# A decoder step for 520 tokens: the input of the S5 layer cut by transposes instead of selection products, the phase tables built in halves, and x loaded once

## What is computed

```python
def _s5_scan(u, h_re, h_im, ...):
    lam_bar = jnp.exp(lam * dt)
    b_bar = ((lam_bar - 1.0) / lam)[..., None] * lax.complex(b_re, b_im)
    ...
        bu = jnp.einsum('blgc,gpc->blgp', u_blk, b_bar)
        bu = bu.at[:, 0].add(lam_bar * h)
        _, hs = lax.associative_scan(_linear_combine, (a, bu), axis=1)
        y = jnp.real(jnp.einsum('blgp,gcp->blgc', hs, c_c)) + d_g * u_blk
...
x = x + mix                      # mixer output, residual
x = x + _hmoe(_rmsnorm(x, norm_ffn), ...)
```

## Time and profile before

| what | us |
|---|---|
| median of 3 runs | 1200.95 (1197.68 to 1205.63) |
| the profiled execution | 1194.14 |
| its span | 1192.3 |
| PE busy | 1025.3 (86%) |
| DVE busy | 431.6 (36%) |
| POOL busy | 333.8 (28%) |
| ACT busy | 169.9 (14%) |

### The profile page before, as it was taken

How to read it: one execution, slowest core, us unless ns; L and a number is a source line. 1 busy time by engine, 2 the same in 40 slices (tenths; PEclk the granted TensorE clock), 3 DMA queues, 4 the chain that set the end, 5 groups by cost and what they waited for, 6 DMA issues and landing times.

```text
span 1192.3 us, 16177 instructions
## 1 busy us (share of the span) xinstructions
PE 1025.3 (86%) x5932; PEld 655.4 (55%) x5932; DVE 431.6 (36%) x939; ACT 169.9 (14%) x320; POOL 333.8 (28%) x550
## 2 busy tenths in 40 slices
PE   3999998899688878888869967999997999877776
PEld 2888877666544444444438865644445555444442
DVE  3300055676542222222373069201346332222216
ACT  3201020132200000000141101200244000000002
POOL 0070000277366666566484000000000112111100
PEclk9999979899599999989985567999997799999999
...
DMA packets 53300, 288.45 MB, mean 242 GB/s; under 512 B 11867, under 2 KB 21851, under 8 KB 34535
## 3 DMA queue, kind: packets, MB, share of 16 engines
...
## 4 chain that ended last, share of the span: by engine, by line
PE 54%; DMA 29%; DVE 7%; SPq 4%; issue 2%; ACT 2%; POOL 1%; DVEq 0%; POOLq 0%; ACTq 0%
DMA arena<-in_w_gu 19%; PE ps L688 12%; PE ps L938 10%; PE ps L815 8%; PE ps L1099 5%; DMA arena<-in_w_down 4%; PE ps L1038 3%; PE ps L1040 3%; PE ps L928 2%; SPq L529 2%; DMA arena<-scratch_yd 2%; DVE arena L1480 2%; PE ps L1070 2%; PE ps L1066 2%; PE ps L845 1%
## 5 line engine op out<-in xcount | busy, mean ns | idle before, releaser
L938 PE MATMUL ps<-arena 128*64 128x256 f32 x2048 | 248.3, 398 | 64.6 <-DMA arena<-in_w_gu 62.7
L938 PEld LDWEIGHTS ps<-arena 128*64 128x64 f32 x2048 | 151.3, 142 | 163.1 <-DMA arena<-in_w_gu 55.4
L2176 POOL TENSOR_TENSOR arena<-arena 128x256 f32<-128x256 f32 (+3 forms) x192 | 132.7, 691 | 40.7 <-POOL arena L2176 40.3
L688 PE MATMUL ps<-arena 128*128 128x260 f32 x640 | 142.8, 383 | 0.0
L2110 POOL TENSOR_TENSOR arena<-arena 128x32 f32<-128x32 f32 (+5 forms) x167 | 90.5, 542 | 161.8 <-ACTq L1273 146.1
L688 PEld LDWEIGHTS ps<-arena 128*128 128x128 f32 x640 | 121.5, 191 | 20.0 <-issue 0.4
L928 PE MATMUL ps<-arena 128*64 128x512 f32 x512 | 118.8, 605 | 13.0 <-DMA arena<-in_w_down 12.5
L815 PE MATMUL ps<-arena 128*128 128x512 f32 x256 | 119.8, 620 | 2.5 <-DVE arena L1626 2.4
L1851 DVE TENSOR_TENSOR arena<-arena,ps 128x128 f32<-128x128 f32 x64 | 18.5, 289 | 276.6 <-ACT arena L1362 271.9
L2207 POOL COPY idx_now<-idx_list 128x1 int32 (+1 forms) x32 | 6.1, 191 | 308.0 <-DVEq L1766 279.5
L815 PEld LDWEIGHTS ps<-arena 128*128 128x128 f32 x256 | 62.4, 251 | 48.4 <-issue 33.0
...
## 6 DMA issues: line engine op xcount, KB each, us to landing
...
```

The costliest lines, as they stand in the source:

```text
L688: mm = pe.matmul(o[:, b, 0:HALF], w[:, kc, (n % 2) * P:(n % 2 + 1) * P], HT[:, kc, b * HALF:(b + 1) * HALF], start=kc == 0, stop=kc == KC - 1)
L938: mm = pe.matmul(ps[CAP * f:CAP * f + CAP, 2 + s, 0:256], XT[l][:, kc, CAP * s:CAP * s + CAP], WGU[l][i][s][:, kc, 256 * f:256 * f + 256], ...
L2176: g_.tensor_tensor(o, x, y, f).then_inc(sem("matrix_steps"), 1)
```

## The change

- x is loaded once, every fourth row to a tile. HT and MIX are written in the order that this asks for (HT with a stride of four elements, MIX in rows of 32 or less), and the output product reads MIX contiguously. The second load and DVE's wait for it go.
- After the experts of layer 0 the tiles are combined in the order 0, 1, 2, samples, 3. ACT makes both block forms and clears a buffer PAD before the first tile. DVE writes the normalised tiles as HX, where the 128 columns of eight groups of four tiles' channels lie together; ACT puts the samples in PAD.
- `recut` and its tables go. PE transposes PAD (16 times) and HX (32 times, in eighths), DVE copies the ends and ACT the middle of U, four copies an eighth. The product `driven` (before: zs) follows each eighth.
- POOL builds the phase table of half 0, reports, waits for the combined sample tile, and builds half 1. R8 is two buffers, filled by ACT after each report.
- SP issues all 8 reads of taps of half 0; those of half 1 are shared with ACT. The last `driven` comes behind the first `columns`. The first half of `glu` of tile 0 comes ahead of the last `turned`.
- `most` is read where it was, by each engine after its loop.

```diff
-    j += [(("k",), "act")]
-    j += [(("u", q), "act" if q % 2 else "dve") for q in range(8)]
-    j += [(("zs", q), "dve") for q in range(8)]
-    for q in range(8):
-        j += [(("y", q), "act" if q < 4 else "dve")]
-        if q >= 2:
-            j += [(("yT", q - 2), "act")]
+    j += [(("k",), "act"), (("us",), "dve"), (("u", 0), "act")]
+    for q in range(4):
+        j += [(("u", q + 1), "act"), (("zs", q), "dve")]
+    j += [(("u", q), "act") for q in (5, 6, 7)] + [(("zs", q), "dve") for q in (4, 5, 6)]
+    j += [(("y", 0), "act"), (("zs", 7), "dve"), (("y", 1), "act")]
+    for q in range(2, 8):
+        j += [(("y", q), "act" if q < 4 else "dve"), (("yT", q - 2), "act")]
...
         HC = place(A + 32928, 5, D)
-        H2 = place(A, 5, D)
+        HX = place(A, GU, TILES, CW)
...
+        R8 = [place(A + 19456 + 1024 * half, PAIRS // 2, NCH) for half in range(2)]
+        TMP = R8[1]
         KS = place(S5_AT, KC, P)
...
+        def norm_of_experts(l, t):
+            if l:
+                return X[:, t, :], HC[:, t, :], GB
+            if t == TILES:
+                return X[:, t, :], HS, GB
+            return by_group(X[:, t, :]), HX[:, :, t, :], by_group(GB)
...
             for i in range(TILES):
-                load(X[:, i, :], T["x_prompt"][i * P:(i + 1) * P, :], f"x_in_{i}")
+                load(X[:, i, :], every_fourth(T["x_prompt"], i), f"x_in_{i}")
...
-            for i in range(TILES):
-                load(X[:, i, :], every_fourth(T["x_prompt"], i), "x_again")
...
-                ring.wait_full(sp, "zs", 4 * half + 3)
-                for s in range(L // 2):
-                    taps(sp, s, half)
+            ring.wait_full(sp, "zs", 3)
+            for s in range(L):
+                taps(sp, s, 0)
+            ring.wait_full(sp, "zs", 7)
+            for s in range(L // 2):
+                taps(sp, s, 1)
...
+                        pe.wait_ge(sem("pad_ready"), 2)
...
+                                 for n in range(GU // 4)])
+            pe.wait_ge(sem("h_2"), 5)
+            rows_of_tiles = HX.rearrange("p g i c -> p (g i c)")
+
+            def in_chunks(q):
+                transposes(("u", q), [(slot("u", q)[:, 0, j * P:(j + 1) * P],
+                                       rows_of_tiles[:, (4 * q + j) * P:(4 * q + j + 1) * P]) for j in range(4)])
+
+            def driven(q):
+                if q == 0:
+                    ring.wait_emptied(pe, "us")
                 ring.wait_free(pe, "zs", q)
                 ring.wait_emptied(pe, "u", q)
...
+
+            in_chunks(0)
+            for q in range(4):
+                in_chunks(q + 1)
+                driven(q)
+            for q in (5, 6, 7):
+                in_chunks(q)
+            for q in (4, 5, 6):
+                driven(q)
+            columns(0)
+            driven(7)
+            for q in range(1, 8):
                 columns(q)
                 if q >= 2:
                     turned(q - 2)
-            for kc in (6, 7):
-                turned(kc)
-            for kc in range(KC):
-                ring.wait_emptied(pe, "yT", kc)
-
...
                     return
-                for kc in range(KC):
+                for kc in kcs:
...
-            for i in range(5):
+                if kcs[-1] == KC - 1:
+                    full(mm)
+            glu(0, range(4))
+            turned(7)
+            glu(0, range(4, KC))
+            for i in range(1, 5):
                 glu(i)
...
-        def phases(tt, m):
+        def phases(tt, half, m):
...
             ur_, ui_ = UNIT[m.bit_length() - 1]
-            c, s = TURNS[:, :, 1], TURNS[:, :, 0]
-            cmul(tt, c[:, :, :, m:2 * m], s[:, :, :, m:2 * m], c[:, :, :, 0:m], s[:, :, :, 0:m], unit(ur_), unit(ui_),
-                 temp(0, m), temp(m, 2 * m))
+            c, s = TURNS[:, half, 1], TURNS[:, half, 0]
+            cmul(tt, c[:, :, m:2 * m], s[:, :, m:2 * m], c[:, :, 0:m], s[:, :, 0:m], unit(ur_), unit(ui_),
+                 TMP[:, :, 0:m], TMP[:, :, m:2 * m])
...
-                give(act, a.copy(HT[:, :, i * P:(i + 1) * P], slot("ht", i).rearrange("p b (k n) -> p (b k) n", n=P)),
+                give(act, a.copy(HT[:, :, i:SEQ:TILES], slot("ht", i).rearrange("p b (k n) -> p (b k) n", n=P)),
                      "ht", i)
...
-                give(act, a.activation(MIX[:, g].rearrange("p (b n) -> p b n", b=2), slot("pw", g)[:, :, 0:HALF],
+                src, first = slot("pw", g), HALF // TILES
+                out = MIX[:, g, 0:SEQ].rearrange("p (i m) -> p m i", i=TILES)
+                step(a.activation(out[:, 0:first], src[:, 0, 0:HALF].rearrange("p (m i) -> p m i", i=TILES),
+                                  ACT.Copy, scale=pscale[:, g:g + 1]))
+                step(a.activation(out[:, first:P], src[:, 1, 0:SEQ - HALF].rearrange("p (m i) -> p m i", i=TILES),
+                                  ACT.Copy, scale=pscale[:, g:g + 1]))
...
+            def clear_pad(step):
+
+                step(a.copy(PAD.rearrange("p g c -> p (g c)"),
+                            before[0:XSROWS, 0:1].broadcast_to((XSROWS, 2 * D))))
+
+            def fill_pad(step):
+
+                rows_ = by_group(HS[0:NS])
+                step(a.copy(PAD[0:NS, :, CW:2 * CW], rows_))
+                a.copy(PAD[XSROWS - NS:XSROWS, :, 0:CW], rows_).then_inc(sem("pad_ready"), 1)
...
-                    tile_squares(act, 2 * l + 2, t, junk[t])
-                    tile_root(act, 2 * l + 2, t, t)
-                    if l == 0 and t < 2:
-                        make_bd(t, step)
+                if l == 0:
+                    for q in range(2):
+                        make_bd(q, step)
+                    clear_pad(step)
+                for k, t in enumerate(combined_order(l)):
+                    act.wait_ge(sem(f"combined_{l}"), k + 1)
+                    tile_squares(act, 2 * l + 2, t, JUNK[l], k)
...
+            def decays(half):
+
+                act.wait_ge(sem("phases_ready"), half + 1)
+                step(a.copy(R8[half], spread(mag8[:, PAIRS // 2 * half:PAIRS // 2 * (half + 1)], NCH)))
+                a.copy(R8[half][:, :, 0:1], zeros.unsqueeze(1).broadcast_to((P, PAIRS // 2, 1))
+                       ).then_inc(sem("decays_ready"), 1)
+
+            def u_out(q):
+                take(act, "u", q)
+                src = slot("u", q)[:, 0, :].rearrange("p (j c s) -> p s j c", j=4, s=2)
+                out = U[:, 8 * q:8 * q + 8].rearrange("p (j b) n -> p b j n", b=2)
+                for b in range(2):
+                    for s in range(2):
+                        ins = a.copy(out[64 * s:64 * s + 64, b, :, NS:SC], src[64 * b:64 * b + 64, s])
+                        if (b, s) != (1, 1):
+                            step(ins)
+                give(act, ins, "u", q)
+
+            for q in range(3):
+                u_out(q)
+            decays(0)
+            for q in range(3, 8):
+                u_out(q)
+            decays(1)
             act.wait_ge(sem("taps_out"), 16)
-            for half in range(2):
-                ring.wait_full(act, "zs", 4 * half + 3)
-                for s in range(L // 2, L):
-                    taps(act, s, half)
+            ring.wait_full(act, "zs", 7)
+            for s in range(L // 2, L):
+                taps(act, s, 1)
...
-                give(dve, v.tensor_tensor(MIX[:, H:2 * H, c * P:(c + 1) * P],
-                                          slot("hT", c)[:, 0, :].rearrange("p (h n) -> p h n", h=H),
-                                          Zo[:, :, c * P:(c + 1) * P], ALU.mult), "hT", c)
+                per = P // TILES
+                out = MIX[:, H:2 * H, 0:SEQ].rearrange("p h (i m) -> p h m i", i=TILES)
+                give(dve, v.tensor_tensor(out[:, :, per * c:per * (c + 1)],
+                                          slot("hT", c)[:, 0, :].rearrange("p (h m i) -> p h m i", h=H, i=TILES),
+                                          Zo[:, :, c * P:(c + 1) * P].rearrange("p h (m i) -> p h m i", i=TILES),
...
-                if k == 0:
-                    dve.wait_ge(sem("x_again"), 16 * TILES)
...
-            recut(dve, step, v.tensor_copy, lambda out, x, m: v.tensor_scalar(out, x, m, None, ALU.mult),
-                  lambda out: step(v.memset(out, 0.0)), 0)
-            ring.wait_full(dve, "u", 7)
+            ring.wait_full(dve, "k")
+            step(v.memset(U[:, :, 0:NS], 0.0))
+            step(v.memset(U[:, :, SC:UC], 0.0))
+            take(dve, "us")
+            src = slot("us")[:, :, 0:8 * XSROWS].rearrange("p b (n k) -> p b n k", k=XSROWS)
+            out = U.rearrange("p (b n g) k -> p g b n k", b=2, n=8)
+            for g_ in range(4):
+                rows_ = src[32 * g_:32 * g_ + 32]
+                step(v.tensor_copy(out[P - 32:P, g_, :, :, 0:NS], rows_[:, :, :, 0:NS]))
+                ins = v.tensor_copy(out[0:32, g_, :, :, SC:UC], rows_[:, :, :, XSROWS - NS:XSROWS])
+                if g_ < 3:
+                    step(ins)
+            give(dve, ins, "us")
```

(24 more changed lines are left out.)

183 lines of the change are left out of this document (80 added, 103 removed).

## The result

The changed kernel takes 1131.76 us (median of four runs, 1126.93 to 1134.85) against 1201.22 for the kernel before on the same chip: a ratio of 0.942, interval 0.937 to 0.946. It is faster by 69 us. The forecast was 1134. The profiled execution took 1131.54, its span is 1129.7; the forecast on that basis was 1127.8.

What follows compares the result with a forecast made beforehand. PE's products making U cost 71.5 us of the chain, around weight-bound expert stages. Terms summed to -66.3: 1194.1 became 1127.8, plus 6.8 for the median over the profiled run, 1134.6, stated as 1134; range 1116 to 1149.

Steps and rivals of the forecast that it cites:

- S: Start of PE's second four eighths of output in the S5 layer: 682.8 us instead of 747.10, -64.3.
- Layer 0: First layer: output product's contiguous weight loads gain 1.2 us, HT's strided write costs 0.5.
- Start of the states: First `rotated` on DVE in the S5 layer: 626 us, POOL's half table and PE level; 629 if half the cover goes.
- Half 0: First half of the S5 states on DVE: 24.8 us as before, ending at 650.8.
- the first rival: POOL and DVE slow each other fully in the S5 layer: second four eighths start at 692, total 1143; chance 0.20.
- Half 1: Second half of the S5 states on DVE: starts at 658 behind POOL's second table, ends at 682.8.
- Taps: SP's and ACT's tap reads for the S5 layer: second half's landing at 673 to 676, covered with 7 us to spare.
- the third rival: Tap reads, not tables, are last: eight take 25 us, halves there at 657 and 692, total 1144; chance 0.10.
- S to the output product: From the second four eighths through GLU: restart at half clock +2.5, reordered transposes -1.3, GLU keeping its clock -2.5.
- full contention: Same as the first rival: POOL and DVE slow each other fully, total 1143; chance 0.20.
- the table bound nothing: Rival on POOL's second phase table: DVE takes POOL's turns, PE binds at 676, total 1125; chance 0.12.
- the slower case: PE stays at 1.2 GHz behind the transposes through GLU and the output product: total 1268; chance 0.03.

Runs made afterwards that it cites:

- e11: The changed kernel as it is, run once more beside the version with all parts: 1129.83 us, ratio 0.942 to the kernel before.
- e2: The changed kernel with POOL waiting for DVE's report of the first half's states before building the second phase table: 1141.50 us, ratio 0.950, one run.
- e9: The changed kernel with POOL's sample terms held until DVE has reported the first half's states: 1123.57 us, ratio 0.938, one run.
- e1: The changed kernel with SP holding the first half's eight tap reads until DVE has reported that half's states: 1148.62 us, ratio 0.956, one run.
- e4: The changed kernel with POOL reporting both halves of its phase table only when both are built: 1147.50 us, ratio 0.954.
- e5: The changed kernel with copies moved from DVE to ACT, last states' products behind the states, and POOL's sample terms after DVE's first report: 1123.49 us, ratio 0.937.
- e6: The changed kernel with the last `driven` product moved ahead of the first `columns`, in PE's order and the PSUM slots: 1129.51 us, ratio 0.943.
- e7: The changed kernel with the edits of e5 and e6 together: 1122.64 us, ratio 0.938.

## Why the prediction was right, and where it was not

The sign, the cause and the size hold: U's products leave PE, and the end moves by what is late next. On the profile basis the sum was -66.3 and the span moved by -62.6. That 1134 came within 2.3 us of the median of 1131.76 is luck in part: the profiled execution missed its 1127.8 by 3.7, and the 6.8 us added because the median of before stood above its profile have no counterpart after (1131.76 and 1131.54). Term by term, taken at four marks (last product of layer 0's experts, S, first product behind GLU, end):

- **Layer 0**, -1.2 + 0.5 forecast. Measured +0.8 (585.99 to 586.77). The write of HT cost 1.6 (between the 0.5 that I took and the bound of 2.2), and ACT's copy of 1024 elements went from 1.02 to 2.06 us. The clock of the gates' product cost 2.5 here and another value in each execution, so that the projections began 4.4 us late (36.17 for 31.78). The output product began 3.4 late and gave about -2, more than the -1.2. At the first product of the experts only 0.3 was left (327.00 for 326.74), since the kernel before waited just ahead of it 1.40 us for a DMA. So the +0.8 is what the waits let through, and not the sum of these terms.
- **Start of the states**, 626 forecast, 628.50 measured; 625.14 in e11. "DVE has only the ends of U to copy, covered by these" did not hold: two memsets and eight copies run from 623.38 to 627.10, and `driven(0)` waited for the last of them. Covered they were only as far as POOL's first table (626.6) ran level. In this execution the third stored tile also came late (the add at 599.36, 12.6 us behind the start of the last expert products, against 9.3 before and 9.4 in e11).
- **Half 0**, 24.8 forecast, 32.3 measured. This is the step that missed by most: "So the bounds are 0 and 11 us on POOL's 27.8, and 0 to 3 on DVE. I take 5". I put the price of sharing on POOL and nearly none on DVE. In truth POOL's 27.8 already held it (20.6 alone), and DVE pays 7.5. The second table, which I made the bound at 658, was ready at 653.5 and bound nothing. Two misses thus offset each other: half 0 ended at 660.8, 10.0 us behind the forecast, but the forecast had half 1 wait until 658 for a table that was there at 653.5, so half 1 began only 3.0 us late. That S came out near its forecast is luck to this extent. e2 shows for both engines that products and scans with both operands in SBUF are slowed, and that products that read PSUM are not (1.42 us for two with and without POOL). By the rule of the Trainium skill that stood with the first rival ("GPSIMD Engine Reference", the table of its interfaces: shared when DVE has two SBUF operands) this was to be expected, and the runs agree with it. The rows of before held a sign of it too. "No POOL form in the earlier trace rows is off its line by more than 0.1 us" rests on 0.899 us for 256 elements, and that is a mean over twelve products: six of the table beside DVE, and six sample terms after 637. The table's six by themselves (before, 590 to 637), and the same form with DVE idle (e2, 649 to 670):

```profile
L2110 POOL TENSOR_TENSOR arena<-arena 128x256 f32<-128x256 f32 x6 | 6.9, 1145 | 0.5
```

```profile
L2175 POOL TENSOR_TENSOR arena<-arena 128x256 f32<-128x256 f32 x6 | 3.9, 650 | 0.5
```

1.145 us stands 0.33 off the 0.81 that the forms beside it gave, and 0.50 above the price alone.
- **Half 1** ends at 686.5 instead of 682.8, nearly all of it inherited.
- **Taps**, "with 7 us to spare for the latter": none was left. `driven(7)` stands behind the first `columns`, which the late half 0 released at 661.02, so it ran at 668.15 and not at 660, and the reads landed at 686.9, by 0.4 us behind DVE. On one queue eight reads take 22 to 24 us (98 GB/s from 640 to 656), near the 25 of the third rival, not 18; in the kernel before sixteen reads of the same size on two queues moved 195 GB/s (712 to 724). The eight of half 1, on two queues, took 17.4. The forecast let eight reads land some 5 us behind the 12.5 us of their issue in the earlier trace rows, where they shared the time with eight of the other queue. Whether the single queue is the reason for the lower rate, no run shows. The reads cost the end little only because DVE was late too.
- **S**: -64.3 forecast, -60.1 measured (687.00 for 747.10), -60.9 without layer 0's shift.
- **S to the output product**: +2.5 - 1.3 - 2.5 forecast, -3.1 measured (82.27 to 79.18 us from S to the end of GLU). The restart at half clock cost 1.5 (first eighth 6.2 us for 4.7); it is not there in every execution (four instructions take 0.63 us at S in e9 behind 2.00 us of waiting, and 1.10 in e11 behind 2.14). GLU's 128 products took 55.3 for 58.19, at 1.00 throughout; what is left, 1.7, is the stretch ahead of GLU with the moved transpose. All three signs right.
- **Behind it** +0.6 in the experts of layer 1 and the last combination, forecast 0.

The rivals: full contention is nearest in mechanism (S at 692, 1143), but with POOL's share priced too high; the table bound nothing, though not for the reason of that rival; the clock came back within 6 us of 661 and within 4 of 687, and the slower case did not come. PE stood at 1.00 from 623 to 642, where the transposes are. So the rule of the Trainium skill ("TensorE: Matmul & The Clock Gate", Part 4), that transposes don't count as activity, cost nothing of the 2 us that I had worked out from it; with `driven` products between them the trace does not contradict it either. The clock is not safe there: in e1, e4, e5, e6 and e7 it fell to 0.51 to 0.58 for 3 to 4 us behind the same first transposes and a wait of 1.8 us (the first or second `driven` took 1.7 to 2.2 us for 1.22), in the other executions it did not at that point.
